# Experts of a mixture in half tiles of 64 rows, two lanes side by side on TensorE's columns

## The reference, cut to what matters

```python
gl = xf @ w_group + b_group;  g = argmax(gl)              # one group of 4
el = einsum('nd,dge->nge', xf, w_erouter) + b_erouter     # its 4 experts
tv, ti = top_k(el[g], 2);     wi = softmax(tv)            # two of them
a = silu(x @ w_gate[g, e]) * (x @ w_up[g, e])             # 1024 -> 256
y = sum over the two of  gate * (a @ w_down[g, e])        # 256 -> 1024
out = rms_norm(x1 + y, g_final)
```

## Time and profile before

| | |
|---|---|
| median of 3 executions | 1259.73 us (1258.3 to 1261.34) |
| the profiled execution | 1258.88 us |
| its span, first instruction to last | 1256.9 us |
| TensorE busy | 1156.9 us, 92% |
| VectorE, ScalarE, GpSimd busy | 56%, 47%, 11% |
| granted clock of TensorE, mean | 0.971 of full speed |
| first gate/up product of the experts | 902.11 us |
| first of the last tile's | 1221.37 us |

### The profile page before, as it was taken

One profiled execution on the slowest core, in us unless ns is written; L12 is line 12 of the kernel. 1 busy time (PEld: TensorE's weight loads), 2 busy tenths in 40 slices (PEclk: granted clock), 3 DMA queues, 4 the chain that ended last, 5 costly groups with the idle time before them and its releaser, 6 DMA issues. The chain is left out here.

```text
span 1256.9 us, 23325 instructions
## 1 busy us (share of the span) xinstructions
PE 1156.9 (92%) x7695; PEld 815.2 (65%) x7695; DVE 698.2 (56%) x1048; ACT 597.1 (48%) x1030; POOL 142.5 (11%) x172
## 2 busy tenths in 40 slices
PE   7999999999688999979999999997689999999992
PEld 5877888888445555544655567875367766667771
DVE  4322112220177776658899977444566666666664
ACT  5520122201176776737568554232155655556654
POOL 1100000000011111100000000000123222433311
PEclk9999999999899999989999999999689999999997
DMA  6642244317599999999999946442679999865476
GB/s 209 218 132 77 82 148 126 101 42 250 189 360 381 345 374 386 382 380 379 383 362 371 387 159 185 155 147 107 245 274 363 375 378 297 239 171 112 101 218 193
DMA packets 155392, 307.43 MB, mean 245 GB/s; under 512 B 22311, under 2 KB 49354, under 8 KB 151178
## 3 DMA queue, kind: packets, MB, share of 16 engines
q1 hardware_dynamic: 145018, 272.38, 60.0%
q0 software_dynamic: 9216, 33.56, 11.5%
q10 hardware_dynamic: 1040, 0.00, 0.0%
HBM read 308.31 MB, written 54.72 MB: 289 GB/s over the span
## 5 line engine op out<-in xcount | busy, mean ns | idle before, releaser
L327 PE MATMUL proj_ps<-w_in_split,x_T_hi 128*128 128x512 f32 x608 | 194.6, 395 | 2.7 <-DVE w_in_split L369 2.7
L2516 DVE TENSOR_TENSOR w_gate_up_split<-w_gate_up,w_gate_up_split 128x2048 fp32r<-128x2048 f32 x62 | 139.3, 2288 | 87.3 <-ACT w_gate_up_split L2574 87.3
L2467 PE MATMUL gate_up_ps<-w_gate_up_split,slot_rows_T 128*128 128x512 f32 x744 | 180.3, 398 | 2.1 <-DVE slot_rows_T L2524 1.9
L2467 PEld LDWEIGHTS gate_up_ps<-w_gate_up_split,slot_rows_T 128*128 128x128 f32 x744 | 139.2, 191 | 31.9 <-DVE slot_rows_T L2524 3.4
L327 PEld LDWEIGHTS proj_ps<-w_in_split,x_T_hi 128*128 128x128 f32 x608 | 115.0, 189 | 27.8 <-DVE x_T_lo L364 2.5
L455 ACT ACTIVATE proj_rows<-proj_ps,sum_squares 128x512 f32<-128x512 f32 x38 | 26.2, 689 | 211.9 <-PE proj_ps L327 200.3
L327 PE MATMUL proj_ps<-w_in_split,x_T_lo 128*128 128x512 f32 x304 | 119.1, 392 | 0.0
L2574 ACT ACTIVATE w_gate_up_split<-w_gate_up 128x2048 fp32r x62 | 115.3, 1912 | 6.7 <-DMA w_gate_up<-in_w_up 5.4
L2489 PE MATMUL expert_out_ps<-w_down,expert_act_T 128*128 x256 | 115.3, 593 | 0.3 <-issue 0.3
L1736 PE MATMUL mix_out_ps<-w_out_split,oT_split 128*128 128x512 f32 x420 | 101.2, 396 | 0.3 <-DVE w_out_split L1875 0.3
L1142 PE MATMUL turns_and_scores_ps<-head_kT,head_qT 64*128 64x512 f32 (+3 forms) x384 | 85.9, 537 | 16.2 <-DMA head_kT<-scratch_kT 9.9
(11 more groups left out here) (255 smaller groups left out, 1750.1 us busy)
## 6 DMA issues: line engine op xcount, KB each, us to landing
w_gate_up<-in_w_gate SPq DMA_DIRECT2D x34, 1024.0 KB, 8.4
w_gate_up<-in_w_up SPq DMA_DIRECT2D x34, 1024.0 KB, 10.2
w_down<-in_w_down SPq DMA_DIRECT2D x34, 1024.0 KB, 12.3
pages<-in_cache_v_d SPq DMA_DIRECT2D x128, 256.0 KB, 5.9
pages<-in_cache_kT_s SPq DMA_DIRECT2D x128, 256.0 KB, 5.7
pages<-in_cache_v_s SPq DMA_DIRECT2D x128, 256.0 KB, 6.0
pages<-in_cache_kT_d SPq DMA_DIRECT2D x100, 256.0 KB, 6.2
w_in_now<-in_w_in SPq DMA_DIRECT2D x48, 256.0 KB, 3.0
```

The lines of the kernel that those rows point to most:

```text
L327: last = pe.matmul(pj_ps[:, n % PJ_BANKS, :], h[:, k, at], w[g % 2][:, k, :], start=(k == 0 and m == 0), stop=(k == KC - 1 and m == 2))
L2467: last = pe.matmul(gu_ps[:, u, :], xT[:, u, a, k, :], gu_split[:, u, b, k, :], start=(k == 0 and m == 0), stop=(k == KC - 1 and m == 2))
L2516: dve.tensor_tensor(gu_split[:, u, 1, at, :].rearrange("p k (c n) -> p k c n", c=2), raw[:, at, :, :], gu_split[:, u, 0, at, :].bitcast(F3 ...
```

## The change

Tiles are halved to 64 rows (`LANE`), at most 2 x 1088 // 64 + 15 = 49 of them. A step takes two, so 25 steps: lane A goes through the half tiles from the first expert up, lane B from the last one down, and they meet in the middle. A step's rows still lie in one tile of 128, lane A's in its first half and lane B's in its second. Lane A's products fill columns 0 to 63 of TensorE and lane B's columns 64 to 127, each with its own expert's weights; both are full fp32, nothing is split. Gate and up weights are one array on the host, so a load is 2 MB. Lane A has four places and reads its weights from them; lane B has two, and each step ScalarE and VectorE copy its weights into one more place (`gu_b`, `dn_b`) from which the products read. The adds are two of 64 rows, each waiting for its own lane's; once lane A's group has reached lane B's they also wait for the other lane's (`add_after`). The first expert of each lane is loaded during `route`.

```diff
-W_PLACES = 4
-W_AHEAD = 2
+LANE = P // 2
+A_PLACES, B_PLACES = 4, 2
-MOE_TILES = (TOP_K * (SEQ + N_SAMPLE) + N_EXPERTS * (P - 1)) // P
+HALF_TILES = TOP_K * (SEQ + N_SAMPLE) // LANE + N_EXPERTS - 1
+MOE_TILES = (HALF_TILES + 1) // 2
...
+                n_halves = ends[:, E - 1:E]
+                link(dve.tensor_tensor(mirror[:, :], wide(n_halves, [P, PAIRS]), part[:, 0, :], ALU.subtract))
+                link(dve.scalar_tensor_tensor(at_step[:, 0, :], mirror[:, :], -1.0, part[:, 0, :], ALU.add, ALU.min))
+                link(dve.tensor_tensor(lane[:, :], part[:, 0, :], at_step[:, 0, :], ALU.is_gt))
+                link(dve.scalar_tensor_tensor(at_step[:, 1, :], lane[:, :], float(LANE), part[:, 1, :], ALU.mult, ALU.add))
...
+                link(dve.tensor_tensor(met[:, :], group_of[:, 0, :], group_of[:, 1, :], ALU.is_ge))
+                for n in range(2):
+                    link(dve.scalar_tensor_tensor(after[:, n, :], t.column[0:1, 0:MOE_TILES], float(n), met[:, :], ALU.add, ALU.mult))
+                link(dve.tensor_scalar(t.add_after[:, :, :], after[:, :, :], 16.0, 16.0, ALU.mult, ALU.max))
...
+                def load_a(tile):
+                    if tile >= MOE_TILES:
+                        return
+                    e, load, at = wanted_load(0, tile)
+                    gu_done.reached(sp, tile - A_PLACES, 1)
+                    own_wait(sp, t)
+                    sp.dma_start(t.gu_a[:, bass.ds(at, 1), :, :].rearrange("p a k n -> p (a k) n"),
+                                 t.w_gu[bass.ds(e, 1), :, :].rearrange("e (p k) n -> p (e k) n", p=P),
+                                 cond=load).then_inc(gu_a_loaded[tile % A_PLACES], 16)
+                    y_done.reached(sp, tile - A_PLACES, 1)
...
+                def load_b(tile):
+                    e, load, at = wanted_load(1, tile)
+                    for half in range(2):
+                        gu_b_kept[half].reached(sp, tile - B_PLACES)
...
+                    for half in range(2):
+                        dn_b_kept[half].reached(sp, tile - B_PLACES)
...
+                load_a(1)
+                for tile in range(1, MOE_TILES):
+                    load_a(tile + 1)
+                    load_b(tile)
...
+                    for n, rows_of in enumerate(lanes):
+                        if tile:
+                            pool.wait_ge(t.added[n], 16 * tile)
+                        if tile or n:
+                            others = pool.value_load(t.add_after[0:1, n, tile:tile + 1], min_val=16, max_val=16 * MOE_TILES)
+                            pool.wait_ge(t.added[1 - n], others)
...
                     for k in range(KC):
                         if k % 4 == 0:
-                            gu_lo.reached(pe, tile, k // 4)
-                        for m, (a, b) in enumerate(PRODUCTS):
-                            last = pe.matmul(gu_ps[:, u, :], xT[:, u, a, k, :], gu_split[:, u, b, k, :],
-                                             start=(k == 0 and m == 0), stop=(k == KC - 1 and m == 2))
-                    last.then_inc(gu_done.sem, 1)
+                            xT_kept[k // 4].reached(pe, tile)
+                            gu_b_kept[k // 4].reached(pe, tile)
+                        pe.matmul(gu_ps[lanes[0], u, :], xT[:, u, k, lanes[0]],
+                                  t.gu_a[:, bass.ds(at, 1), k, :].rearrange("p a n -> p (a n)"),
+                                  start=(k == 0), stop=(k == KC - 1))
+                        last = pe.matmul(gu_ps[lanes[1], u, :], xT[:, u, k, lanes[1]], gu_b[:, k, :],
+                                         start=(k == 0), stop=(k == KC - 1))
+                        if k % 4 == 3:
+                            last.then_inc(gu_done.sem, 1)
...
                 for tile in range(MOE_TILES):
-                    if tile + 1 < MOE_TILES:
-                        split_gu(tile + 1)
                     swish(tile)
...
                     if tile + 1 < MOE_TILES:
-                        split_rows(tile + 1)
+                        keep_rows(tile + 1)
+                        take_gu(tile + 1)
                     keep_act(tile)
                     if tile:
                         keep_y(tile - 1)
+                    take_dn(tile)
```

More of the change, by code:

```diff
@@ L2240, in _ @@
                     sp.wait_ge(t.h_stored[u], 16 * len(range(u, TILES, 2)))
-                for e in range(W_AHEAD):
-                    load_ahead(sp, t, e)
+                load_first(sp, t)
             @block.tensor
@@ L2432, in _ @@
                         add_rows(tile - behind)
-                pool.wait_ge(t.added, 16 * MOE_TILES)
+                for n in range(2):
+                    pool.wait_ge(t.added[n], 16 * MOE_TILES)
                 pool.wait_ge(normed, 1)
@@ L2442, in turn_rows @@
                     for half in range(2):
-                        xT_kept.reached(pe, tile - 1, half)
+                        xT_kept[half].reached(pe, tile - 1)
                         for k in range(4):
@@ L2479, in down @@
                 def down(tile, halves=(0, 1)):
-                    u, at = tile % 2, place(pe, tile)
+                    u, at = tile % 2, place(pe, 0, tile)
                     aT_kept.reached(pe, tile)
-                    pe.wait_ge(dn_loaded[tile % W_PLACES], 16 * (tile // W_PLACES) + 16)
-                    if tile < W_AHEAD:
-                        pe.wait_ge(t.w_ahead[tile], 48)
+                    if tile:
+                        pe.wait_ge(dn_a_loaded[tile % A_PLACES], loads(tile, A_PLACES))
+                    if tile < A_PLACES:
+                        pe.wait_ge(t.first_dn[0], 16)
+                    for half in range(2):
+                        dn_b_kept[half].reached(pe, tile)
                     for c in halves:
@@ new lines, in take_dn @@
+                def take_dn(tile):
+                    at = place(dve, 1, tile)
+                    if tile:
+                        dve.wait_ge(dn_b_loaded[tile % B_PLACES], loads(tile, B_PLACES))
+                    if tile < B_PLACES:
+                        dve.wait_ge(t.first_dn[1], 16)
+                    y_done.reached(dve, tile - 1, 1)
+                    own_wait(dve, t)
+                    dve.tensor_copy(dn_b[:, 1:2, :], t.dn_b[:, bass.ds(at, 1), 1:2, :].rearrange("p a k n -> p (a k) n"))\
+                       .then_inc(dn_b_kept[1].sem, 1)
@@ L2603, in keep_y @@
                     if tile >= 2:
[L2604 removed]
+                        for n in range(2):
+                            act.wait_ge(t.added[n], 16 * (tile - 1))
                     act.activation(y[:, u, 0:BANK], y_ps[:, 0, :], ACT.Copy, scale=t.slot_gate[:, tile:tile + 1])\
                        .then_inc(y_kept[0].sem, 1)
[L2608 to L2609 removed]
+                take_gu(0)
+                keep_rows(0)
                 for tile in range(MOE_TILES):
[L2611 to L2612 removed]
                     swish(tile)
@@ L2636, in _ @@
             def _(pool):
-                for one in [one for one in sems if one not in passed_by_all] + t.rows_loaded + t.x1_loaded + [t.added]:
+                for one in [one for one in sems if one not in passed_by_all] + t.rows_loaded + t.x1_loaded + t.added:
                     pool.sem_clear(one)
@@ L2724, in step_kernel @@
         expert_places(nc, ctx, t)
-        with ExitStack() as parts:
-            t.gu_split = parts.enter_context(nc.sbuf_tensor("w_gate_up_split", [P, 2, 2, KC, GU], F32R))
-            stage(t, route, nc, t)
-            stage(t, experts, nc, t)
+        stage(t, route, nc, t)
+        stage(t, experts, nc, t)
         t.held.close()
```

346 lines of the change are left out of this document (189 added, 157 removed).

## The result

The change makes the kernel slower. It takes 1284.1 us (median of 4 runs, 1282.8 to 1286.3), the kernel before on the same chip 1260.5: a ratio of 1.018, 95% interval 1.0167 to 1.0197. The forecast was 1241, so 43 us are to be found. The profiled execution of after has a span of 1282.2 us, against the 1238.6 of the forecast's sum.

A forecast was written before the change was run, and what follows sets the result against it. TensorE was taken to bound the expert stage, the chain of adds close behind. Start 930.7 + 22 steps of 11.8, 10 of waits, the tail and 1 for adds gave a span of 1238.6, forecast 1241 us; range 1225 to 1262.

The forecast's parts named there:

- Lanes side by side, copies hidden: Expert step: gate/up takes 16 slots, 6.88 us; ScalarE's and VectorE's weight copies stay off the path, 1.9 us slack.
- (d): Expert steps: the lanes run one after the other, 258 us more, 1499; chance 0.03 together with (e).
- (e): Expert steps: weight loads not hidden, 6.6 us a step, 165 in all, 1406; chance 0.03 together with (d).
- Change of form: Expert step: switching between 64-column halves and whole 128 columns costs 0.1 us each, 0.4 a step, 0.14 at most.
- the sum: Step parts 6.88 + 0.87 + 3.44 + 0.22 + 0.4 = 11.8 us; whole span 1238.6 us, with 10 of waits.
- Lane B's weights arrive late: Expert stage: waits of 0 to 5 us at lane B's five expert changes, taken as 2 each, 10 in all.
- Adds: Expert stage and tail: two 64-row adds per step, chains merging from step 18, latency 4.5 us; 1 us taken.
- T(24) + 14 L - 37.0: Tail: landing time of the last of fourteen merged adds at latency L; T(24)+26 at 4.5 us.
- (c): Merged adds become the bound from a latency of 5.3 us; 1248 at 5.8, typically 1268; chance 0.09.
- (b): Expert stage: lane B's weights come later, 4 to 5 us each time, 1254; chance 0.18.
- Route and start: Route +2.1 us and lane B's first copy +1.4 before the first gate/up; then step 0 takes 12.4, step 1 12.7.
- T0: Start of the first gate/up in the expert stage, forecast at 905.6 us.

The follow-up runs named there:

- lane A alone: Lane B's products left out but each sum's first, against the changed kernel with earlier lane B gate/up loads and no cross-lane add waits in dead steps: 1243.4 us.
- the order with two changes: TensorE does down before turned rows, against the changed kernel with earlier lane B gate/up loads and no cross-lane add waits in dead steps: 1241.3 us.

## Why the prediction was wrong, point by point

*Lanes side by side, copies hidden (right).* 16 pairs of 0.43 us, as read from the earlier trace rows; rivals (d) and (e) are out, by the pairs and by lane A alone. ScalarE's copy took 1.91 us and VectorE's 1.3. In steps without new weights nothing waits for them.

*Change of form (right in kind, mis-sized).* A step took 11.99 and not 11.8. Between the starts of the groups stand 7.02 us for gate/up, 1.02 for the turned rows, 3.58 for down and 0.37 for the turned activations; over the 6.88, 0.87, 3.44 and 0.22 of the sum, each is 0.14 or 0.15 more. In the order with two changes, gate/up followed by down is 6.91, 0.03 over the sum, so most of that 0.14 goes with the change of form. The excess is the upper bound taken from the earlier trace rows, where I took 0.1: 4 us. The Trainium skill (TensorEngine Tiling (Array Packing), Key Properties) states the drain, and the four gaps agree.

*Lane B's weights arrive late (the step that failed).* The mechanism was named and the issue was placed rightly, at T + 2.4 to 2.7 of the step before. What failed was the landing, and then the price. The 7.7 us were built from the first megabytes ahead of the stage, where the other queue carried nothing; in after the first 2 MB there landed 7.9 us behind their issue. In the stage, with 0.3 MB of adds on the other queue, the same 2 MB needed 8.9 us to the last packet and 9.8 to ScalarE's start. And for the 1 MB of lane A ahead in the queue I had up to 2.6 us; with it and up to 0.3 MB of A's gate/up weights it was 12.3 to 14.2 us, 2.5 to 4.4 more than without. I had worked out landings of 7.7 to 10.3 us against some 7.6 of slack and then took 2 us for each change. The waits on TensorE's path were 5.2, 7.0, 2.4, 6.8 and 2.4.

*What a wait does to the clock (missing).* During the longest wait, ahead of 1056.83, TensorE stood for 6.96 us, and the granted clock was at half, the lower of its two levels (1.2 GHz, not 2.4), from 1053.7 on and still when TensorE went on. From 985 to 993, in the end of tile 6's wait and behind it, it was 0.57, and pairs came 0.86 us apart at first instead of 0.43. Four gate/up groups took 1.3 to 2.4 us longer for it, 7.2 in all. Behind 928 us, shows TensorE busy and at the full clock, so nothing there could give a price. But the first stretch, at 0.83, holds one: the trace of before has a wait of 3.25 us in it, the granted clock is 0.50 from 914.2 to 920.8, and the gate/up behind takes 8.31 us, where the others take 5.73:

```profile
914.19 0.69 PE L2476 MATMUL act_T_ps<-ident,expert_act 128*128 128x128 f32 x2 [3.25 <-DVE expert_act L2531]
915.39 8.31 PE L2467 MATMUL gate_up_ps<-w_gate_up_split,slot_rows_T 128*128 128x512 f32 x24 [0.50 <-DVE slot_rows_T L2524]
```

That is 2.6 us more; behind the waits of after it was up to 2.4.

*Adds (the second step that failed).* From step 18 on the chains do merge, and the line for the last landing, T(24) + 14 L - 37.0, comes close: the last fourteen adds took 5.4 us each in the mean, which puts the landing at T(24) + 38.7, and it was at T(24) + 42.6, since the next add was issued 0.9 us behind a landing and not 0.7, and the first of them 0.8 us late. In the line's terms the latency is 5.7 us, where I took 4.5. But it was compared with the end of the span (T(24) + 37.3), not with the last moment at which an add may land. Behind the last landing the span goes on for 10.6 us of clearing and draining on GpSimd; before it was 9.0 (landed at 1247.9, end at 1256.9), so it could have been read. With it the chain decides from (37.0 + 37.3 - 10.6) / 14 = 4.6 us on and not from 5.3, and at 5.7 the end moves by 16 us. Rival (c) put +7 us at a latency of 5.8. Less the 1 us that the sum had for it, these are the 14.9 of the table.

*Rivals and range.* The result is (b) and (c) at once, each beyond its price: (b) stopped at 5 us each with no cost in clock, and (c) left the 10.6 us out. Taken as alternatives, they were never added up, and so 1284 lay above the range.

*Route and start (right).* 0.3 us from the route's first operation to T0, 12.7 instead of 12.4 for step 0.

## What to carry to other kernels

When a load is placed in a step, write down the whole queue ahead of it at its issue, in bytes, other lanes' loads and other queues' traffic included, and price its landing from transfers in the same company; if the slack comes out within a few us of the landing, issue it a step earlier, which here was worth 29 us, and look at what then stands behind it (one load of lane A came 1.6 us late). Find for each chain that ends the kernel the last moment at which it may end, by reading what follows the same event in the profile of before. A wait of TensorE can cost more than its length (four of five did here), and risks that share one execution are to be added, not weighed against each other.

## What the hardware showed that was not expected

- One queue moved its loads one behind the other (16 KB, 4 KB, 16 KB, 4 KB packets), with an overlap of 1.9 to 4.0 us where the engines were out of step. In after a 2 MB load needed 9.8 us from issue to use with nothing ahead, and 12.3 to 14.2 with 1.1 to 1.3 MB ahead.
- A load can end on a few engines: in the kernel with the later down load the DMA share fell to 0.47 over 3.5 us at the end of one, with 5, then 3, then 1 of its packets in flight.
- The granted clock fell to half within the three waits of TensorE of 5 to 7 us, and the gate/up groups behind them took up to 9.4 us instead of 7.02. Of the two waits of 2.4 us one was followed by 5 us at a mean of 0.66, the other by the full clock.
- From the last add's landing to the end of the span it takes 9.0 us before, 10.6 after and 10.9 with the adds of dead steps paired. GpSimd's drain is 5.2 us of it before and 6.1 in the other two.
- 64-row adds, 256 KB, landed after 4.4 us at the least and 6.9 in the middle of all fifty, where 128 rows took 5.8 and 7.2. With no weights loading, the last fourteen took 4.8 in the middle, and the last thirteen of 128 rows 6.2: half of the bytes, three quarters of the time.
